# Compressed-attention stage of a hybrid decoder layer: pages laid two tokens to a partition, split by head in pieces, keys and values worked apart, first fetches moved ahead of the stage

## The reference

```python
def compress_blocks(kv, cmp_pe, cmp_w):
    B, L = kv.shape[:2]                       # kv (B, L, 2, G, dh)
    n_cmp = (L - BLOCK_CMP) // STRIDE_CMP + 1  # 32-token blocks, every 16 tokens
    r = BLOCK_CMP // STRIDE_CMP
    n_chunks = n_cmp + r - 1
    chunks = kv[:, :n_chunks * STRIDE_CMP].reshape(B, n_chunks, STRIDE_CMP, 2, N_KV_HEADS, HEAD_DIM)
    pe = cmp_pe.reshape(2, r, STRIDE_CMP, HEAD_DIM)
    w = cmp_w.reshape(2, r, STRIDE_CMP, HEAD_DIM, HEAD_DIM)
    comp = 0.0
    for i in range(r):
        part = chunks[:, i:i + n_cmp] + jnp.moveaxis(pe[:, i], 0, 1)[None, None, :, :, None, :]
        comp = comp + jnp.einsum('bnscgd,csde->bncge', part, w[:, i])
    return comp[:, :, 0], comp[:, :, 1], c_end
```

## Time and profile before

| | us |
|---|---|
| median of 3 runs (lowest, highest) | 2737.37 (2721.35, 2755.52) |
| the profiled execution: its time, its span | 2724.35, 2722.6 |
| PE busy in the span | 2351.4 (86%) |
| `rw_all_done`, by POOL's first instruction behind it | 827.1 |
| first PE instruction of prompt attention | 1024.3 |
| sample attention, about | 1353 to 1557 |

### The profile page before, as it was taken

One profiled execution on the slowest core, in us unless ns is written; L12 is line 12 of the kernel. 1 busy time (PEld: TensorE's weight loads), 2 busy tenths in 40 slices (PEclk: granted clock), 3 DMA queues, 4 the chain that ended last, 5 costly groups with the idle time before them and its releaser, 6 DMA issues.

```text
span 2722.6 us, 37448 instructions
## 1 busy us (share of the span) xinstructions
PE 2351.4 (86%) x15820; PEld 1321.1 (49%) x15820; DVE 804.9 (30%) x1750; ACT 559.6 (21%) x1292; POOL 170.2 (6%) x253
## 2 busy tenths in 40 slices
PE   8999899888874696877755589899999999999999
PEld 4464445787863573333322334454454445444543
DVE  2046333556551237765433201101110111111101
ACT  4024331222211124655512212100000000000000
POOL 2000000222201111111100000000000000000000
PEclk9998889999985897999977799899999999999999
DMA  5000003000005530000033330101011010101000
GB/s 156 17 8 23 24 16 120 3 11 11 3 4 87 98 111 1 1 1 1 23 117 109 85 141 27 62 0 62 3 59 62 0 62 0 62 0 62 0 31 35
DMA packets 84726, 115.75 MB, mean 43 GB/s; under 512 B 30899, under 2 KB 68724, under 8 KB 83406
## 3 DMA queue, kind: packets, MB, share of 16 engines
q1 hardware_dynamic: 84558, 113.35, 13.9%
HBM read 104.75 MB, written 12.64 MB: 43 GB/s over the span
## 4 chain that ended last, share of the span: by engine, by line
PE 75%; DVE 7%; DMA 5%; SPq 4%; ACT 4%; issue 3%; POOL 0%; POOLq 0%; DVEq 0%; ACTq 0%
PE psum L1121 71%; DMA arena<-in_cache_cmp_kv_dram 3%; SPq L612 2%; DVE arena L2067 2%; SPq L580 2%; PE psum L1524 1%; ACT arena L1028 1%; PE psum L1581 1%; DVE arena L1934 1%; ACT arena L1014 1%; DVE psum L2062 1%; DMA arena<-in_w_out_dram 1%; SPq L596 1%; PE psum L1461 1%; DMA arena<-in_w_up_dram 0%
## 5 line engine op out<-in xcount | busy, mean ns | idle before, releaser
L1121 PE MATMUL psum<-arena 64*64 64x64 f32 (+11 forms) x12912 | 2089.1, 353 | 177.3 <-ACT arena L1028 53.8
L1121 PEld LDWEIGHTS psum<-arena 64*64 64x64 f32 (+5 forms) x12912 | 1088.7, 156 | 1079.1 <-issue 891.3
L1115 ACT ACTIVATE arena<-psum 128x512 f32<-128x512 f32 (+1 forms) x96 | 45.4, 473 | 837.7 <-PE psum L1121 837.7
L2199 DVE TENSOR_TENSOR arena<-arena 128x512 f32<-128x512 f32 (+1 forms) x96 | 51.5, 537 | 455.9 <-ACT arena L1115 455.9
L2208 DVE TENSOR_TENSOR arena<-arena,psum 128x512 f32<-128x512 f32 (+1 forms) x72 | 49.4, 685 | 449.9 <-PE psum L1121 449.9
L1581 PE MATMUL psum<-ident,arena 128*128 128x128 f32 (+1 forms) x248 | 47.7, 337 | 80.3 <-DMA arena<-in_cache_slc_kv_dram 74.4
L731 POOL TENSOR_TENSOR arena<-arena,m_lev 128x256 f32<-128x256 f32 x82 | 67.3, 821 | 684.9 <-DVE arena L1915 440.2
L1014 ACT ACTIVATE arena<-psum 128x512 f32<-128x512 f32 (+1 forms) x148 | 80.6, 595 | 95.2 <-PE psum L1524 81.6
L1028 ACT ACTIVATE arena<-psum,arena 128x640 f32<-128x640 f32 (+7 forms) x128 | 89.6, 701 | 30.9 <-DVE arena L2067 28.8
L2067 DVE TENSOR_REDUCE arena<-psum 128x1 f32<-128x640 f32 (+7 forms) x128 | 90.6, 708 | 4.4
L1461 PE MATMUL psum<-ident,arena 128*128 128x128 f32 (+1 forms) x288 | 46.8, 293 | 46.4 <-DVE arena L2017 46.4
(11 more groups left out here) (281 smaller groups left out, 1218.1 us busy)
## 6 DMA issues: line engine op xcount, KB each, us to landing
arena<-in_cache_cmp_kv_dram SPq DMA_DIRECT2D x128, 128.0 KB
arena<-in_cache_slc_kv_dram SPq DMA_DIRECT2D x128, 128.0 KB, 2.3
arena<-in_w_down_dram SPq DMA_DIRECT2D x4, 4096.0 KB, 13.7
arena<-in_w_up_dram SPq DMA_DIRECT2D x4, 4096.0 KB, 13.6
arena<-in_x_prompt_dram SPq DMA_DIRECT2D x16, 512.0 KB, 9.4
arena<-in_w_in_dram SPq DMA_DIRECT2D x13, 512.0 KB, 3.8
arena<-in_w_in_dram SPq DMA_DIRECT2D x2, 2048.0 KB, 14.6
arena<-in_cache_win_kv_dram SPq DMA_DIRECT2D x8, 512.0 KB, 5.0
```

What stands on the lines that cost most here:

```text
L1121: return nc.tensor.matmul(out, lhsT, rhs, start=start, stop=stop)
```

## The change

- **Layout.** A page lands as 64 partitions of two tokens (2 KB each), pages with even numbers on the lower 64 partitions and odd on the upper. A sequence takes four pieces of 128x1024 (`page_rows[k % 2][x]`, each 4 pages), in the space of the recurrence's columns. The prompt's rows come as four DMAs of 128x512.
- **Order of sequences.** `CSEQ`: sample sequence 0 first, then the prompt, then the other seven.
- **Sorting by head.** POOL's copy is gone. DVE does all of it, in pieces of 128x512 (`split_heads`), keys (a = 0) and values (a = 1) apart, two halves ahead of PE.
- **Transposes and products.** A piece gives 4 transposes of 128x128 to one bank. The copy to `xt` now reads the bank with a step of 8 elements and writes runs of 32. The unit of work is a half (one sequence, keys or values): 8 matmuls, with the next half's four groups of transposes between them, and the selection of the half before after the fourth.
- **Early fetches.** SP reads the first 16 page numbers, and fetches the weights when the last value columns of the recurrence are read (`rw_vt`), and the first sequence's pages when `F_PR0` is (`rw_w`). The bias matmuls stand in PE's list in period 18 of the recurrence, and so do the state transposes, now ahead of the last output's.
- **`vb`** is made by POOL, and its 8 matmuls stand ahead of PE's wait for `nub`.
- **Page numbers** are read without the bounds `min_val` and `max_val`, in both attention stages.
- The gates' arithmetic on ACT and DVE moves from the stage's head into its loop. The weights lie where `vnew` is loaded, so SP waits for the last product before loading `vnew`.

```diff
-        chunk_flat = [work(STRIDE * 2 * D_KV) for _ in range(2)]
-        by_head = work(2 * KVH, STRIDE, HD)
-        xt = [work(2, KVH, P) for _ in range(2)]
-        assert at[0] <= W0
+        HSTR = STRIDE // 2
         at[0] = W1
-        xt += [work(2, KVH, P) for _ in range(2)]
         ycmp = work(2, KVH, P)
-        wcmp = work(2, STRIDE // 2, 2, HD)
-        pecol = work(2, 2, STRIDE // 2)
         pebias = work(2)
+        xt = [work(HSTR, KVH, P) for _ in range(2)]
         assert at[0] <= W_END
+        wcmp = [shaped(v, HSTR, 2, HD) for v in (vnew_flat[:, 0:D_MODEL], vnew_flat[:, D_MODEL:])]
+        pecol = shaped(ft[:, F_L, 0:4 * HSTR], 2, 2, HSTR)
+        page_rows = [[ft[:, slot + x, 0:SEQ] for x in range(HP)] for slot in (F_PR0, F_K)]
+        by_head = [[ft[:, F_R + x, c0:c0 + 512] for x in range(HP)] for c0 in (512, 0)]
...
+            def page(b, n):
+                return sp.value_load(pages[0:1, b * NPG + n:b * NPG + n + 1])
+            def load_pages(k, at_page):
+                for n in range(NPG):
+                    src = cache_cmp_kv[0, bass.ds(at_page[n], 1)].rearrange("o (c s) a g d -> (o c) (s a g d)", s=2)
+                    t = n // 2
+                    sp.dma_start(page_rows[k % 2][t // 2][HALVES[n % 2], 512 * (t % 2):512 * (t % 2) + 512], src).then_inc(sem(f"pages_in{k % 2}"), 16)
+            def page_numbers(u):
+                return [page(u - 1, n) for n in range(NPG)]
+            first = page_numbers(CSEQ[0])
+            sp.wait_ge(sem("rw_vt"), NCH + 1)
+            with nc.allow_non_contiguous_dma("256-byte runs of the compression weights"):
+                for c in range(2):
+                    for i in range(2):
+                        sp.dma_start(wcmp[c][:, :, i, :], cmp_w[0, c, i * STRIDE:(i + 1) * STRIDE].rearrange(
+                            "(sp s) d e -> (s d) sp e", s=2)).then_inc(sem("wcmp_in"), 16)
+                        sp.dma_start(pecol[:, c, i, :], cmp_pe[0, c, i * STRIDE:(i + 1) * STRIDE].rearrange(
+                            "(sp s) d -> (s d) sp", s=2)).then_inc(sem("wcmp_in"), 16)
+            sp.wait_ge(sem("rw_w"), NCH)
+            load_pages(0, first)
...
-            def page(b, n):
-                return sp.value_load(pages[0:1, b * NPG + n:b * NPG + n + 1], min_val=0,
-                                     max_val=cache_cmp_kv.shape[1] - 1)
-            def load_chunks(u):
-                at_page = [page(u - 1, n) for n in range(NPG)] if u > 0 else []
-                if u >= 2:
-                    sp.wait_ge(sem("cm_rows"), u - 1)
-                    sp.wait_ge(sem("cm_krows"), u - 1)
-                flat = chunk_flat[u % 2]
-                if u == 0:
-                    sp.dma_start(flat[0:SEQ // STRIDE, :], prompt_cmp[0, 0].rearrange(
-                        "n (c s) a g d -> (n c) (s a g d)", s=STRIDE)).then_inc(sem("chunk_in0"), 16)
-                    return
-                rows_of_page = PAGE // STRIDE
-                for n in range(NPG):
-                    src = cache_cmp_kv[0, bass.ds(at_page[n], 1)].rearrange("o (c s) a g d -> (o c) (s a g d)", s=STRIDE)
-                    sp.dma_start(flat[n * rows_of_page:(n + 1) * rows_of_page, :], src).then_inc(sem(f"chunk_in{u % 2}"), 16)
...
+            for k in range(1, NSEQ):
+                if CSEQ[k] == 0:
+                    for t in range(SEQ // (2 * P)):
+                        dst = page_rows[k % 2][t // 2][:, 512 * (t % 2):512 * (t % 2) + 512]
+                        sp.dma_start(dst, prompt_cmp[0, 0, 2 * t:2 * t + 2].rearrange(
+                            "n (c s) a g d -> (n c) (s a g d)", s=2)).then_inc(sem(f"pages_in{k % 2}"), 16)
+                    continue
+                numbers = page_numbers(CSEQ[k])
+                if k >= 2:
+                    sp.wait_ge(sem("cm_heads"), gbase(k - 1, 0))
+                load_pages(k, numbers)
+            sp.wait_ge(sem("cm_mm"), len(CHALF))
...
+            pool.wait_ge(sem("rw_vgsb"), NCH + 1)
+            pool.wait_ge(sem("rw_tok"), NCH)
+            for hp in range(HP):
+                ins = nc.gpsimd.tensor_tensor(vb[:, hp], spread(vtok_r[NCH % 3][:, hp, :], 1, DEC_B), spread(row_of, 2, HD), ALU.mult)
+            ins.then_inc(once("rw_vb")[0], 1)
...
-                nc.gpsimd.tensor_copy(*head_rows(u, 1)).then_inc(sem("cm_rows"), 1)
...
+                nc.scalar.activation(xt[a][:, :, :, 32 * x:32 * x + 32],
+                                     shaped(banks[g % 4], KVH, 32, HSTR).rearrange("p k c s -> p s k c"), ACT.Copy).then_inc(sem("cm_x1"), 1)
...
+                    if c == NCH:
+                        pe.wait_ge(*once("rw_vb"))
+                        for hp, q in enumerate(SBANK):
+                            for h in HALVES:
+                                mm(banks[q][h, :], tokbk[h, 1, hp, :], vb[h, hp, :, :].rearrange("p a b -> p (a b)"), True, False)
...
+                if n == NCH + 2 and k == 9:
+                    pe.wait_ge(sem("wcmp_in"), 16 * 8)
+                    for c in range(2):
+                        for sp_ in range(HSTR):
+                            ins = mm(banks[5][:, 2 * c:2 * c + 2], wcmp[c][:, sp_].rearrange("p a b -> p (a b)"), pecol[:, c, :, sp_],
+                                     sp_ == 0, sp_ == HSTR - 1)
+                    ins.then_inc(once("pe_sum")[0], 1)
+                    pe.wait_ge(sem("rw_st"), NCH + 1)
+                    for b in range(DEC_B):
+                        if b >= 2:
+                            pe.wait_ge(sem("rw_sstate_rows"), b - 1)
+                        for hp in range(HP):
+                            ins = nc.tensor.transpose(banks[b % 2][0:64, hp * P:(hp + 1) * P], sst[:, hp, b, :], ident)
+                        ins.then_inc(sem("rw_sstate"), 1)
...
+            def cm_turn(k, a, x):
+                g = gbase(k, a) + x
+                pe.wait_ge(sem("cm_heads"), g + 1)
+                if g >= 4:
+                    pe.wait_ge(sem(f"cm_x{g % 2}"), (g - 4) // 2 + 1)
+                for kv in range(KVH):
+                    for t in range(2):
+                        cols = slice((2 * kv + t) * P, (2 * kv + t + 1) * P)
+                        ins = nc.tensor.transpose(banks[g % 4][:, cols], by_head[a][x][:, cols], ident)
+                ins.then_inc(sem("cm_turned"), 1)
+            def cm_product(k, a, sp_):
+                n = chunks(k)
+                if sp_ == 0:
+                    last = gbase(k, a) + cgroups(k)
+                    pe.wait_ge(sem("cm_x0"), last // 2)
+                    pe.wait_ge(sem("cm_x1"), last // 2)
+                    if k > 0:
+                        pe.wait_ge(sem("cm_y"), 2 * (k - 1) + a + 1)
+                ins = mm(shaped(banks[4 + a][:, 0:KVH * n], KVH, n), wcmp[a][:, sp_].rearrange("p a b -> p (a b)"),
+                         xt[a][:, sp_, :, 0:n], sp_ == 0, sp_ == HSTR - 1)
+                if sp_ == HSTR - 1:
...
+            for x in range(cgroups(0)):
+                pe.wait_ge(sem("kt_ready"), x + 1)
+                cm_turn(0, 0, x)
+            pe.wait_ge(sem("kt_ready"), 5)
+            pe.wait_ge(*once("pe_bias"))
+            for j, (k, a) in enumerate(CHALF):
+                for sp_ in range(HSTR):
+                    if sp_ % 2 == 0 and j + 1 < len(CHALF) and sp_ // 2 < cgroups(CHALF[j + 1][0]):
+                        cm_turn(*CHALF[j + 1], sp_ // 2)
+                    cm_product(k, a, sp_)
+                    if sp_ == 3 and j >= 1:
+                        cm_select(*CHALF[j - 1])
+            cm_select(*CHALF[-1])
...
-                            tt(nub[:, hp], spread(nu[:, hp, :], 1, DEC_B), rowm, ALU.mult)
-                            ins = tt(vb[:, hp], spread(vtok_r[r][:, hp, :], 1, DEC_B), rowm, ALU.mult)
+                            ins = tt(nub[:, hp], spread(nu[:, hp, :], 1, DEC_B), rowm, ALU.mult)
...
+            def split_heads(k, a, x):
+                if x == 0 and a == 0:
+                    dve.wait_ge(sem(f"pages_in{k % 2}"), pages_landed(k))
+                if k > 0:
+                    dve.wait_ge(sem("cm_turned"), gbase(k - 1, a) + min(x + 1, cgroups(k - 1)))
+                tokens = shaped(page_rows[k % 2][x], 4, 2, KVH, HD)[:, :, a]
+                nc.vector.tensor_copy(shaped(by_head[a][x], KVH, 4, HD).rearrange("p g t d -> p t g d"), tokens).then_inc(sem("cm_heads"), 1)
+            def x_copy(k, a, x):
+                g = gbase(k, a) + x
+                dve.wait_ge(sem("cm_turned"), g + 1)
+                if k > 0:
+                    dve.wait_ge(sem("cm_mm"), 2 * (k - 1) + a + 1)
+                nc.vector.tensor_copy(xt[a][:, :, :, 32 * x:32 * x + 32],
+                                      shaped(banks[g % 4], KVH, 32, HSTR).rearrange("p k c s -> p s k c")).then_inc(sem("cm_x0"), 1)
+            for x in range(cgroups(0)):
+                split_heads(0, 0, x)
...
+            for x in range(0, cgroups(0), 2):
+                x_copy(0, 0, x)
+            dve.wait_ge(sem("stored"), 16 * stores[1])
```

(16 more changed lines are left out.)

192 lines of the change are left out of this document (66 added, 126 removed).

## The result

The changed kernel takes 2639.33 us (median of 4 runs, 2634.16 to 2644.64) against 2735.26 for the kernel before (4 runs, 2721.35 to 2755.52): ratio 0.9663, 95% interval 0.9622 to 0.9704. The forecast was 2622 in a range of 2595 to 2668. Executions more than 1.5% above the fastest of their kernel are left out of every ratio in this document. The profiled execution took 2644.64 us with a span of 2642.9, 80 us under the span before; the forecast for the profiled execution was 108.

A forecast was written before the change was run, and what follows sets the result against it. It took page DMAs to bound two thirds of the stage from the recurrence's end to prompt attention, and PE its end. Savings of 88 us there and 20 in sample attention made 108: 2616 us profiled, 2622 as median, range 2595 to 2668.

## What to carry to other kernels

When a stage is fed by many small DMAs with computed addresses, add up the issuing queue's own list, number reads and issues, for each unit of work, and hold it against the pitch of the engine that it feeds; what does not fit goes to a second queue or into a time when the queue waits. Don't interpolate the price of an issue between shapes: measure the one that is meant. And where a DMA share stands still at a round fraction while the rate moves, as here at 0.50 to 0.51, ask whether it is a part of the engines, full.

## What the runs showed of the chip that I had not expected

- The issue on SP costs 277 ns for 8 neighbouring partitions of 16 KB, 645 for 8 that stand 4 apart, 316 for 32 of 4 KB, 468 for 64 of 2 KB, 333 for 128 of 1 KB. It grows neither with the partitions nor with the size of a piece; what in the shape decides it stays open.
- ACT issues the 64-partition page in 476 ns, about as SP does (468), and POOL in 518.
- The bounds of one register read cost 0.27 us on SP: 0.56 with, 0.294 without.
- In 860 to 885 us a busy DMA engine moved 9.0 GB/s into 8 neighbouring partitions, 20.8 into 8 that stand 4 apart, 15.3 into 32 neighbours, 18.3 and 18.5 into 64 and 128. The 9.0 is no constant: it rose to 22.1 by 965 to 995 us, in the same kernel and with the same shape.
